# Retention in a two-layer hybrid encoder: rotary partner rows by DMA inside SBUF, re-centered values in another PSUM bank

## The reference

```python
def rotary(x, pos):
    half = x.shape[-1] // 2                      # 32 of 64
    cos, sin = ...                               # of pos * inv
    x1, x2 = x[..., :half], x[..., half:]
    return concatenate([x1 * cos - x2 * sin, x1 * sin + x2 * cos], -1)

def retention(q, k, v, g, gn_g):                 # 4 heads, q and k of 64, v of 128
    q, k = rotary(q), rotary(k) * 64 ** -0.5
    scores = einsum(q, k) * decay_in             # inside a chunk
    y = einsum(scores, v) + q_decay * (q @ R_prev)
    # R: running state of k (decayed) times v
    yn = (y - mean(y)) * rsqrt(var(y) + EPS) * gn_g
    return silu(g) * yn
```

## Time and profile before

| | us |
|---|---|
| median of 3 runs | 1334.67 (1334.59 to 1341.18) |
| the profiled execution | 1339.34 |
| its span, first to last instruction | 1337.6 |
| granted TensorE clock, mean | 0.993 |

### The profile page before, as it was taken

How to read it: one execution, slowest core, us unless ns; L and a number is a source line. 1 busy time by engine, 2 the same in 40 slices (tenths; PEclk the granted TensorE clock), 3 DMA queues, 4 the chain that set the end, 5 groups by cost and what they waited for, 6 DMA issues and landing times.

```text
span 1337.6 us, 21561 instructions
## 1 busy us (share of the span) xinstructions
PE 1296.2 (97%) x6130; PEld 1042.3 (78%) x6130; DVE 634.7 (47%) x957; ACT 627.4 (47%) x961; POOL 577.7 (43%) x433
## 2 busy tenths in 40 slices
PE   6999999999999999999999999999999999999995
PEld 4777777777888888888877777777788888888884
DVE  6845567366444203443267546664744430144423
ACT  6432285356666323333363225825676652233433
POOL 2533344154444544444444334333454444444443
PEclk9999999999999999999999999999999999999998
DMA  6334222132333322332223432121323333223232
GB/s 193 111 104 111 64 79 76 35 103 79 102 94 94 110 95 84 97 99 95 98 81 104 118 87 79 58 69 55 103 88 101 100 97 101 95 94 94 94 103 102
DMA packets 77305, 125.32 MB, mean 94 GB/s; under 512 B 7672, under 2 KB 20248, under 8 KB 77112
## 3 DMA queue, kind: packets, MB, share of 16 engines
q1 hardware_dynamic: 77240, 124.47, 30.2%
HBM read 121.89 MB, written 2.55 MB: 93 GB/s over the span
## 4 chain that ended last, share of the span: by engine, by line
PE 81%; DVE 10%; issue 5%; ACT 2%; DVEq 1%; DMA 0%; ACTq 0%; SPq 0%
PE dense L924 74%; PE mix L924 6%; DVE arena L674 2%; DVE h_lo L607 2%; DVE ssq L613 1%; ACT w_hi L418 1%; PE mix L1095 1%; DVE arena L696 1%; DVE arena L769 0%; DVE arena L671 0%; DVE pad L664 0%; DMA x<-in_xT 0%; DVE mx L799 0%; DVE arena L805 0%; DVE arena L872 0%
## 5 line engine op out<-in xcount | busy, mean ns | idle before, releaser
L359 POOL TENSOR_TENSOR w_lo<-w_raw,w_hi 128x512 fp32r<-128x512 f32 x428 | 577.3, 1365 | 749.7 <-ACT w_hi L418 735.0
L924 PE MATMUL dense<-h_hi,w_hi 128*128 128x512 f32 x1152 | 458.1, 398 | 14.8 <-ACT w_hi L405 6.3
L924 PE MATMUL dense<-h_lo,w_hi 128*128 128x512 f32 x1152 | 450.8, 391 | 0.0
L418 ACT ACTIVATE w_hi<-w_raw 128x512 fp32r<-128x512 f32 x424 | 249.3, 622 | 186.1 <-PE dense L924 181.3
L924 PE MATMUL dense<-h_hi,w_lo 128*128 128x512 f32 x1152 | 309.8, 391 | 0.0
L924 PEld LDWEIGHTS dense<-h_hi,w_hi 128*128 128x128 f32 x1152 | 217.7, 189 | 67.7 <-issue 14.1
L924 PEld LDWEIGHTS dense<-h_lo,w_hi 128*128 128x128 f32 x1152 | 217.6, 189 | 46.7 <-issue 2.5
L924 PEld LDWEIGHTS dense<-h_hi,w_lo 128*128 128x128 f32 x1152 | 217.4, 189 | 45.7
L924 PE MATMUL dense<-m_hi,w_hi 128*128 128x512 f32 x544 | 217.3, 400 | 3.2 <-ACT w_hi L418 2.5
L924 PE MATMUL dense<-m_lo,w_hi 128*128 128x512 f32 x544 | 211.9, 390 | 0.0
L924 PE MATMUL dense<-m_hi,w_lo 128*128 128x512 f32 x544 | 146.8, 389 | 0.0
(11 more groups left out here) (160 smaller groups left out, 990.8 us busy)
## 6 DMA issues: line engine op xcount, KB each, us to landing
w_raw<-in_w SPq DMA_DIRECT2D x428, 256.0 KB, 2.6
arena<-cum_rows SPq DMA_DIRECT2D x8, 512.0 KB, 6.3
x<-in_xT SPq DMA_DIRECT2D x8, 256.0 KB, 5.5
out_y<-arena SPq DMA_DIRECT2D x8, 256.0 KB, 2.2
arena<-exp_rows SPq DMA_DIRECT2D x12, 128.0 KB, 7.0
consts<-in_consts SPq DMA_DIRECT2D x1, 1283.0 KB
rel_scratch<-arena SPq DMA_DIRECT2D x1, 382.0 KB
bias<-rel_scratch SPq DMA_DIRECT2D x8, 32.0 KB, 2.0
```

The lines of the kernel that those rows point to most:

```text
L359: nc.gpsimd.tensor_tensor(w_lo[:, s, :], w_raw[:, s, :], w_hi[:, s, :].bitcast(f32), ALU.subtract).then_inc(lo_ready, 1)
L418: nc.scalar.activation(w_hi[:, slot, :], w_raw[:, slot, :], ACT.Copy).then_inc(hi_ready, 1)
L924: return T.matmul(dst, lhsT, rhs, start=start, stop=stop)
```

## The change

Four things, all in the retention:

- The step RP has no part on TensorE any more, and `perm` leaves the constants. Instead SP copies the partner rows inside SBUF: for each of the four tiles four DMAs of [32, 512], 16 per layer, into new tiles `k_part` (where `css` lay) and `q_part` (new in the arena). They stand on SP's queue between packs 43 and 44, behind three waits: for SB3's two banks and for the evacuation of the last q tile (unit 15).
- VectorE multiplies the copied rows with the sines in place, waits for that operation's end, multiplies the tile with the cosines, waits, and adds. The sign sits in the sine table. It waits for the 16 copies, and no longer for the RP before, the SSD's normalization or bank 4.
- RV uses bank 3 instead of bank 5.
- RB doesn't wait for the last RV any more.

```diff
@@ BANKS
-    "AS": (0, 1, 4), "AT": (2, 3), "AV": (2,), "RP": (4,), "RV": (5,), "SN": (4,),
+    "AS": (0, 1, 4), "AT": (2, 3), "AV": (2,), "RV": (3,), "SN": (4,),
@@ arena
+_a = lay("qart", _a, 4 * KB)
+lay("part", OFF["cs"][0], 4 * KB)
@@ SP, per layer
                 spread(3)
-                weights(8, N_PACKS // SLOTS)
+                weights(8, 10)
+                sp.wait_ge(m_ready[4], ready("SB3", 1, l))
+                sp.wait_ge(m_ready[5], ready("SB3", 2, l))
+                sp.wait_ge(evac, l * N_UNITS + U_RQ + 4)
+                for t in range(4):
+                    src = (rk if t < 2 else rq)[:, t % 2, :]
+                    dst = (k_part if t < 2 else q_part)[:, t % 2, :]
+                    for r in range(0, P, 32):
+                        other = r ^ 32
+                        sp.dma_start(dst[r:r + 32, :], src[other:other + 32, :]).then_inc(part_loaded, 16)
+                weights(10, N_PACKS // SLOTS)
@@ ScalarE, RV
-                        act.wait_ge(m_ready[5], ready(name, 0, l))
-                        nc.scalar.activation(vtok[:, :, n, :], bank(5, 4), ACT.Copy).then_inc(m_free[5], 1)
+                        act.wait_ge(m_ready[3], ready(name, 0, l))
+                        nc.scalar.activation(vtok[:, :, n, :], bank(3, 4), ACT.Copy).then_inc(m_free[3], 1)
@@ VectorE, RP
-                        if n:
-                            dve.wait_ge(rot_done, l * 4 + n)
-                        else:
-                            dve.wait_ge(gn_done, l * 4 + 4)
-                        dve.wait_ge(m_ready[4], ready(name, 0, l))
-                        V.tensor_tensor(rot[:, :], M[4][:, :], consts["sin"][:, :], ALU.mult)\
-                            .then_inc(m_free[4], 1)
+                        pr = (k_part if n < 2 else q_part)[:, n % 2, :]
+                        dve.wait_ge(part_loaded, l * 256 + 256)
+                        link(V.tensor_tensor(pr, pr, consts["sin"][:, :], ALU.mult))
                         link(V.tensor_tensor(r, r, consts["cos"][:, :], ALU.mult))
-                        dve.wait_ge(m_free[4], ready(name, 0, l) + 1)
-                        V.tensor_tensor(r, r, rot[:, :], ALU.add).then_inc(rot_done, 1)
+                        V.tensor_tensor(r, r, pr, ALU.add).then_inc(rot_done, 1)
@@ TensorE, RP
-                    elif step == "RP":
-                        r = (rk if n < 2 else rq)[:, n % 2, :]
-                        pe.wait_ge(evac, l * N_UNITS + U_RK + n + 3)
-                        take(name, 0, l)
-                        mm(M[4][:, :], perm[:, :], r).then_inc(m_ready[4], 1)
@@ TensorE, RV
-                            ins = mm(M[5][:, P * b:P * b + P], pad[:, (U_RV + n) % 2, at:at + BLK], center[:, :])
-                        ins.then_inc(m_ready[5], 1)
+                            ins = mm(M[3][:, P * b:P * b + P], pad[:, (U_RV + n) % 2, at:at + BLK], center[:, :])
+                        ins.then_inc(m_ready[3], 1)
@@ TensorE, RB
-                        pe.wait_ge(m_free[5], ready("RV3", 0, l) + 1)
@@ constants
-CONSTS = {"ident": P, "ones": P, "center": P, "perm": P, "lastsel": P, ...
+CONSTS = {"ident": P, "ones": P, "center": P, "lastsel": P, ...
-    c["sin"] = np.tile(np.sin(ang.astype(np.float64)), (4, 1)).astype(f)
+    sin = np.sin(ang.astype(np.float64)).astype(f)
+    c["sin"] = np.concatenate([-sin, sin, -sin, sin], 0)
```

More of the change, by code:

```diff
@@ L115 @@
 ACT_LINKS = 5
-DVE_LINKS = 83
+DVE_LINKS = 87
 KB = 256
@@ L188, in build @@
         pad = sb("pad", [P, 2, 4 + S])
-        rot = rs = ssq
+        rs = ssq
         rs2 = (ssq, rstd)
@@ L192, in build @@
         consts, par = pieces(c_all, CONSTS), pieces(p_all, PARAMS)
-        ident, ones, center, perm = (consts[n] for n in ("ident", "ones", "center", "perm"))
+        ident, ones, center = (consts[n] for n in ("ident", "ones", "center"))
         by_head = sb("by_head", [8, 2 * DEPTH])
@@ L227, in build @@
         rk, rq = ar("rk", 2), ar("rq", 2)
+        k_part, q_part = ar("part", 2), ar("qart", 2)
         vtok = ar("vtok", NB, 4)
@@ L266, in build @@
         a_hi, a_lo = sem("att_hi"), sem("att_lo")
-        rot_done = sem("rot_done")
+        rot_done, part_loaded = sem("rot_done"), sem("part_loaded")
         qd_done, y_sum = sem("qd_done"), sem("ssd_y_summed")
@@ L638, in _ @@
                         if U_RV + 2 <= n < U_RV + 6:
-                            dve.wait_ge(m_ready[5], ready(f"RV{n - U_RV - 2}", 0, l))
+                            dve.wait_ge(m_ready[3], ready(f"RV{n - U_RV - 2}", 0, l))
                         if n in U_RG[2:]:
@@ L1190, in _ @@
             norm(2 * DEPTH, "NORM", DEPTH)
-CONSTS = {"ident": P, "ones": P, "center": P, "perm": P, "lastsel": P, "causal": P, "cos": S, "sin": S,
+CONSTS = {"ident": P, "ones": P, "center": P, "lastsel": P, "causal": P, "cos": S, "sin": S,
           "decin": 4 * P, "qdec": 2 * P, "kdec": 4, "gch": 2}
@@ L1223, in constants @@
          "center": (np.eye(P) - 1.0 / P).astype(f)}
[L1224 to L1228, removed]
     last = np.zeros((P, P), f)
```

## The result

| kernel | median us (lowest to highest) | runs | mean granted clock |
|---|---|---|---|
| before | 1336.48 (1334.59 to 1341.18) | 8 | |
| changed | 1345.62 (1343.93 to 1350.40) | 8 | 0.989 |

The ratio is 1.0063 with a 95% interval of 1.0048 to 1.0079: the change makes the kernel about 9 us slower. Forecast was 1334.9, in a range of 1329 to 1339. The clock column is the mean, over the executions, of the granted clock that each run lists; over the 62 executions of the kernel before that the later comparisons took, it is 0.994.

A forecast was written before the change was run, and what follows sets the result against it. TensorE was taken as the bound, with VectorE late at RA0 once the products go. Per layer -1.3 + 0.5 + 0.9 = +0.1, two layers +0.2 us on the median 1334.67: forecast 1334.9, range 1329.0 to 1339.0.

The forecast's parts named there:

- The bank: RV in bank 3: 1.3 us a layer gained at RV0, 0.5 us of new wait at AT0.
- The rotary stage: VectorE's rotary steps up to RA0: RA0 0.9 us later a layer, with four products gone from TensorE.
- Step 1: VectorE's rotary step 1: starts at about 225.05 instead of 224.51, 0.5 us later.
- The two times 1 us lost to GpSimd: Two GpSimd operations, behind units 28 and 29, delay VectorE's rotary steps by about 0.95 and 0.75 us.
- 2.8 against 2.75 hold in any order: VectorE's rotary step with evacuation takes 2.8 us, TensorE's dense unit 2.75: VectorE can't keep up, even undisturbed.
- the cover: Pack 44 on SP's queue: delayed to 166.7, ScalarE wants it at 168.89; delay hidden with 2 us of cover.
- My own threshold: SP's queue: packs 44 and 45 come late if one copy takes more than 0.59 us to issue.
- rival 3: SP queue: packs 44/45 late above 0.59 us per issue; 0.6 to 1.0 us a layer at 0.63; chance 0.12.
- the SP term: Sixteen DMAs on SP's queue at 0.45 us per issue, 7.2 us in all: hidden, costed at nothing.

The follow-up runs named there:

- e4_spread: The changed kernel with the rotary steps moved up in the schedule, only VectorE's order differing: 1337.05 us, ratio 0.9989 to the kernel before.
- e3_psum: The changed kernel with VectorE's sine product reading PSUM bank 4 instead of the copied rows, rotation not computed: 1345.70 us, ratio 1.0039 to before.
- e7_three1: The kernel before with three TensorE waits of 1.0 us per layer added in the MLP's first down projection: 1346.49 us, ratio 1.0056.

## Where the prediction was right and where it failed

**Right, in place and size.** The bank: 1.3 us forecast at RV0, 1.21 and 1.34 found; 0.5 at AT0, 0.44 and 0.47 found. The rotary stage: RA0 was to be 0.9 us later with all four products gone; the ledger has -0.87 + 1.55 = +0.68. Step 1 starts 0.4 us later than before in the frame of TensorE at that place (forecast 0.5), the chain from there takes 9.4 us (9.6), unit 30 and RA0 wait 3.75 us together (about 4). The two times 1 us lost to GpSimd were forecast as 0.95 and 0.75.

**Wrong inside that.** I counted 0.80 us for an operation and the wait for its own end. In the changed kernel such a pair starts 0.71 to 0.73 us apart where GpSimd is not in the way (223.98, 224.69, 225.42). A step with its evacuation is therefore 2.65 us and not 2.8 (230.63 to 233.28 in VectorE's rows of the changed kernel), less than a dense unit's 2.75. By these rows VectorE alone would keep up; it is GpSimd that makes it late. The bound "2.8 against 2.75 hold in any order" was wrong, and e4_spread shows the same work hidden entirely.

**Failed: the DMAs on SP's queue, costed at nothing.** I took 0.45 us per issue, nearer the plain weight load, and called the cover 2 us. The issue took 0.59 us and 0.63 with what lies between two, the upper of my two rows. My own threshold was 0.59, and the price that rival 3 gave for 0.63 us was 0.6 to 1.0 us a layer; measured are 1.32 and 1.36. The argument that the dear rows have three levels or a broadcast was what misled: a copy of 32 rows of 2 KB costs as much.

**Failed, and the larger part: the clock had no term at all.** I wrote down a wait of 3.75 us ahead of RA0 and unit 30 and priced it by its length. The trace of the kernel before had a fall to show it, at the wait of 2.5 us near 64 us in layer 0, and I had read its mean clock as a constant. That wait, and the window behind it:

```profile
PE dense L924 <- DVE arena L664: 2.5, 1, 2.5
...
64.00:68.00 4.00, 3.87 (x10) 3.10 (x11) 3.36 (x6) 0.00 (x0) 0.38 (x1) 0.57 0.41 131
```

With four waits of 2.0 to 2.7 us per execution that the kernel before doesn't have, the mean clock went from 0.994 to 0.989, 6.8 us. With it and the SP term the sum would have been 0.2 + 2.7 + 6.8 = 9.7, near the measured 9.1, with the reserve on the 6.8 that is made above.

The exclusion of VectorE and GpSimd, which I drew from the Trainium skill ("SBUF — State Buffer", section "Who interferes with whom"), held as it stands there: operations with two SBUF sources took 1.65 to 1.73 us beside GpSimd's, the one from PSUM 0.67. What I took from it too quickly was that the source of one product is the matter; e3_psum shows that the next operation pays.

## What to carry over

Work taken off the busiest engine is worth its time only if the engine that feeds the next step keeps up: write down the other engine's time for the same stretch, with what it loses to a neighbour, and move its part to where it idles (one line of the schedule was worth 9 us here). Price a new wait of TensorE at its length plus what follows it. Here a wait of 1.0 us cost 1.2 us, one of 2.2 us with a fall of the clock 4.0 us, one of 2.8 us 4.4 to 4.6 us. Several short ones are cheaper than one long one of the same sum. DMAs put ahead of a prefetch on the same queue cost their issue, by number and not by bytes: issue few large ones.

## What the runs showed of the hardware

- A DMA inside SBUF of 32 rows took SP 0.59 us to issue, with 2 KB per row as with 4 KB, against 0.33 us for a weight load of 128 rows of 2 KB from memory. It landed in 2.0 us (median).
- Behind a wait of TensorE of 2.0 to 2.8 us the granted clock fell to 1.2 GHz for 3.4 to 6.8 us, in some executions and at some of the places (14 of 22 in the traces, without the two such waits that every kernel has); behind the six added waits of 1.0 us it did not fall. At one place it fell behind a wait of 0.4 us, in 5 of 13 traces. Mean clocks: 0.9941 before in the same groups, 0.9902 with two waits of 2.2 us, 0.9892 with two of 2.8 us, 0.9938 with six of 1.0 us. What decides in a single execution stays open.
- The unit behind a wait of 0.97 us took 1.21 us more (e7_three1), 0.24 us beyond the wait itself.
- VectorE's wait for its own end cost 0.11 to 0.13 us more than plain succession, where both operations read SBUF alone (0.72 against 0.60).
